# Float32r products whose columns are taken in blocks of sixteen from both halves of the operand in turn

## The chip, the cores and the metric

The kernel runs on one core of a Trainium2 chip. The metric is the time of one execution on the device, in microseconds (us). The core has five engines that run side by side and meet only through semaphores: TensorE (PE in the profile; its weight loads are listed apart, as PEld), VectorE (DVE), ScalarE (ACT), GpSimd (POOL) and SyncE (SP), which issues the transfers.

## The reference

What is computed is a stack of transformer blocks over 256 tokens of width 1024, all in float32. A first block has two layers: one with a gated linear recurrence (`hgrn2_mixer`), one with differential attention (`diff_attn_mixer`), each followed by a squared-ReLU feed-forward of width 4096. A second block has one layer: a mixer that joins a low-rank attention with a short gated convolution, a gated feed-forward of width 2816, and a gated embedding. Nearly all arithmetic is in products of this kind:

```python
def squared_relu_mlp(h, w_up, w_down):
    u = jax.nn.relu(h @ w_up)
    return (u * u) @ w_down

# second block, one layer
h = rmsnorm(x, mix_pre_norm[i])
z = h @ w_in[i]
...
f = (jax.nn.silu(h @ w_gate[i]) * (h @ w_up[i])) @ w_down[i]
x = x + rmsnorm(f, ffn_post_norm[i])
```

## The kernel before

**How a product is computed.** Every weight matrix is read from memory once, in pieces of 128 rows by 1024 columns that land in `w_raw` (4 buffers). ScalarE rounds a piece to the type float32r (`w_hi`, L1424), and VectorE subtracts to get what the rounding left over (`w_lo`, L1990); both have 5 buffers. The activations are kept in the same two parts side by side: in `xs` (and in `us`, `xs_b`, `xs_m`, `xs_s`, which serve other stages) one tile of 128 rows has 512 columns, of which the first 256 are the high parts of the 256 tokens and the last 256 the low parts. A product of a 128x128 tile of weights with the tokens is then three products of float32r: high weights by high tokens, high weights by low tokens, and low weights by high tokens. The three are added up in PSUM (`ps`, 8 banks of 512 columns). A float32r product has 256 or 512 columns; TensorE loads the 128x128 stationary operand ahead of each one.

**The forms of it.** `quantum` is the inner piece. For most layers (`kind == "feat"`) the high-weight products stand in two forms: `both_halves` (L649) takes all 512 columns with one weight load, `one_half` (L657) takes the two halves of 256 columns one after the other with two weight loads. L660 is the low-weight product. How many of the high-weight products are 512 wide is set by the table `WIDE` (L226). The other kinds, "direct" (L676 to L678), "one_bank" (L682 to L684), "one_bank_tok" (L689 to L691) and "tok" (L695 to L697), have 256 columns only. In the tok kinds the operands change places: the tokens are stationary, and the weights are the moving operand. `high_records` and `low_records` (L609, L610, L617) serve the first units of a stage. `short_tile` (L1143 to L1145), the products of `kr` (L1130 to L1132), of `ukv` (L1189 to L1191) and of `ple` (L1270 to L1272) are the same three products on other operands. The built program has 6162 float32r products of 256 columns and 579 of 512 that read their columns in a row.

**Other products.** Sums of squares, scores and turned tiles are products of plain float32: L826, L904, L917, L936, L949 to L952 are such. The profile has two records for each, since the engine passes over it twice, and each record has a weight load of its own. Two of them don't read their columns in a row: L917 reads `hq_both` in pairs or singly, with jumps, and writes with steps of 2 or 4 columns into PSUM; L936 reads runs of 4, 8 or 16 columns with as many left out between them.

**Where the operands lie.** A tensor starts at a multiple of 64 bytes, and most tensors are a multiple of 128 bytes long. `w_hi`, `w_lo`, `h` and `mo` start at an even multiple of 64 bytes. Ahead of `xs` stands a gap of 64 bytes (`HALF_PERIOD`), so that `xs` starts at an odd multiple; so do all tensors of the arena: `us`, `xs_b`, `xs_m`, `xs_s`, and also `hk`, `hq_both`, `ple_hi` and `ple_lo`. A product's first column is always at a multiple of 512 bytes from its tensor's start.

```python
w_hi = sb("w_hi", [P, SLOTS, QCOLS], F32R)
w_lo = sb("w_lo", [P, SLOTS, QCOLS], F32R)
h = sb("h", [P, KT, S])
top[0] += HALF_PERIOD
xs = sb("xs", [P, KT, 2 * S], F32R)
top[0] += HALF_PERIOD
mo = sb("mo", [P, KT, S])
```

**What sets the order.** The order of each engine's work is written out by hand. TensorE goes through the list `STREAM` unit by unit; it waits for the converted weights (`lo_ready`), for the tokens (`xs_ready`, `xs_hi`) and for PSUM banks to be taken (`pair_summed`). When it is done with a buffer it counts up `w_used`, which lets ScalarE and VectorE convert the next piece, and so the next transfer start.

Of the kernel before, what the change touches and what calls it, by code (L numbers as in the profile page):

```python
# [17 lines left out]
P = 128  # L18
D = 1024
S = 256  # L20
KT = D // P
# [207 lines left out]
def layered_kernel(nc, a, out):  # L229

    ctx = ExitStack()
    with ctx:
# [14 lines left out]
        w_hi = sb("w_hi", [P, SLOTS, QCOLS], F32R)  # L247
# [352 lines left out]
        def _(pe):  # L600
            mm = nc.tensor.matmul

            def high_records(s, kt, x, kind, pset):

                hi, lo = (w[:, s, kt % 4 * 2 * P:(kt % 4 + 1) * 2 * P] for w in (w_hi, w_lo))
                for n in range(2):
                    w = slice(n * P, (n + 1) * P)
                    o_ap = ps[:, 2 * pset + n, 0:S] if kind == "feat" else ps[:, pset, n * S:(n + 1) * S]
                    mm(o_ap, hi[:, w], x[:, kt, 0:S], start=kt == 0 and (kind == "feat" or n == 0), stop=False)  # L609
                    mm(o_ap, lo[:, w], x[:, kt, 0:S], start=False, stop=False)  # L610

            def low_records(s, kt, x, kind, pset):

                hi = w_hi[:, s, kt % 4 * 2 * P:(kt % 4 + 1) * 2 * P]
                for n in range(2):
                    o_ap = ps[:, 2 * pset + n, S:2 * S] if kind == "feat" else ps[:, pset, n * S:(n + 1) * S]
                    o = mm(o_ap, hi[:, n * P:(n + 1) * P], x[:, kt, S:2 * S], start=False,  # L617
                           stop=kt == KT - 1 and (kind == "feat" or n == 1))
                return o

# [20 lines left out]
            def quantum(s, kt0, nk, last_kt, x, kind, pset, kk0=0, tiles=(0, 1), wide=0, wide_first=False):  # L641

                hi, lo = w_hi[:, s, :].rearrange("p (k n) -> p k n", k=4), w_lo[:, s, :].rearrange("p (k n) -> p k n", k=4)
                if kind == "feat":
                    steps = [(kk, n) for kk in range(kk0, kk0 + nk) for n in tiles]

                    def both_halves(some):
                        for kk, n in some:
                            o = mm(ps[:, 2 * pset + n, :], hi[:, kk, n * P:(n + 1) * P], x[:, kt0 + kk, :],  # L649
                                   start=kt0 + kk == 0, stop=kt0 + kk == last_kt)  # L650
                        return o

                    def one_half(some):
                        for kk, n in some:
                            for half in range(2):
                                at = slice(half * S, (half + 1) * S)
                                mm(ps[:, 2 * pset + n, at], hi[:, kk, n * P:(n + 1) * P], x[:, kt0 + kk, at], start=False,  # L657
                                   stop=False)
                        for kk, n in steps:
                            o = mm(ps[:, 2 * pset + n, 0:S], lo[:, kk, n * P:(n + 1) * P], x[:, kt0 + kk, 0:S], start=False,  # L660
                                   stop=False)
                        return o

                    if wide_first:
                        both_halves(steps[:wide])
                        return one_half(steps[wide:])
                    one_half(steps[:-wide])
                    return both_halves(steps[-wide:])
                for kk in range(kk0, kk0 + nk):
                    kt = kt0 + kk  # L670
                    first, last = kt == 0, kt == last_kt
                    for n in tiles:
                        bank = 2 * pset + n
                        if kind == "direct":
                            w = slice(n * P, (n + 1) * P)
                            mm(ps[:, bank, 0:S], hi[:, kk, w], x[:, kt, 0:S], start=first, stop=False)  # L676
                            mm(ps[:, bank, 0:S], hi[:, kk, w], x[:, kt, S:2 * S], start=False, stop=False)  # L677
                            o = mm(ps[:, bank, 0:S], lo[:, kk, w], x[:, kt, 0:S], start=False, stop=last)  # L678
                        elif kind == "one_bank":
                            w = slice(n * P, (n + 1) * P)  # L680
                            at = slice(n * S, (n + 1) * S)
                            mm(ps[:, pset, at], hi[:, kk, w], x[:, kt, 0:S], start=first and n == 0, stop=False)  # L682
                            mm(ps[:, pset, at], hi[:, kk, w], x[:, kt, S:2 * S], start=False, stop=False)  # L683
                            o = mm(ps[:, pset, at], lo[:, kk, w], x[:, kt, 0:S], start=False, stop=last and n == 1)  # L684
                        elif kind == "one_bank_tok":
                            xh = x[:, kt, n * P:(n + 1) * P]
                            xl = x[:, kt, S + n * P:S + (n + 1) * P]
                            at = slice(n * S, (n + 1) * S)
                            mm(ps[:, pset, at], xh, hi[:, kk, :], start=first and n == 0, stop=False)  # L689
                            mm(ps[:, pset, at], xh, lo[:, kk, :], start=False, stop=False)  # L690
                            o = mm(ps[:, pset, at], xl, hi[:, kk, :], start=False, stop=last and n == 1)  # L691
                        else:
                            xh = x[:, kt, n * P:(n + 1) * P]
                            xl = x[:, kt, S + n * P:S + (n + 1) * P]
                            mm(ps[:, bank, 0:S], xh, hi[:, kk, :], start=first, stop=False)  # L695
                            mm(ps[:, bank, 0:S], xh, lo[:, kk, :], start=False, stop=False)
                            o = mm(ps[:, bank, 0:S], xl, hi[:, kk, :], start=False, stop=last)  # L697
                return o

            def first_two(name, x, waits, mid=None):  # L700
# [422 lines left out]
            for part in range(2):  # L1123
                g0 = 2 * UNIT0["kr"] + part
                pe.wait_ge(lo_ready, g0 + 1)
                khi, klo = (w[:, g0 % SLOTS, :].rearrange("p (k n) -> p k n", k=4) for w in (w_hi, w_lo))
                for kk in range(4):
                    kt = 4 * part + kk
                    o_ap = ps[:, MIX_BANK["kr"], 0:S]
                    mm(o_ap, khi[:, kk, 0:P], xs[:, kt, 0:S], start=(kt == 0), stop=False)  # L1130
                    mm(o_ap, khi[:, kk, 0:P], xs[:, kt, S:2 * S], start=False, stop=False)
                    o = mm(o_ap, klo[:, kk, 0:P], xs[:, kt, 0:S], start=False, stop=(kt == KT - 1))  # L1132
                o.then_inc(w_used, 1)

            sums("mix_pre")
# [4 lines left out]
            def short_tile(name, kt, cols, bank, n, xi, first, last):  # L1140
                s = (2 * UNIT0[name] + kt) % SLOTS
                o_ap, xk = ps[:, bank, n * S:(n + 1) * S], xs_s[:, xi + kt, :]
                mm(o_ap, w_hi[:, s, cols], xk[:, 0:S], start=first, stop=False)  # L1143
                mm(o_ap, w_hi[:, s, cols], xk[:, S:2 * S], start=False, stop=False)
                return mm(o_ap, w_lo[:, s, cols], xk[:, 0:S], start=False, stop=last)  # L1145

            pe.wait_ge(xs_ready, XS0["cq"] + 1)
            pe.wait_ge(lo_ready, 2 * UNIT0["uq"] + 2)
# [33 lines left out]
            for m in range(2):  # L1182
                if m == 1:
                    pe.wait_ge(z_dve, BY_DVE["uq3"])
                for kt in range(2):
                    s = (2 * UNIT0["ukv"] + kt) % SLOTS
                    xh, xl = (xs_s[:, 2 + kt, S * i + m * P:S * i + (m + 1) * P] for i in range(2))
                    o_ap, cols = ps[:, UV_BANK[m], :], slice(AH * NOPE, QCOLS)
                    mm(o_ap, xh, w_hi[:, s, cols], start=(kt == 0), stop=False)  # L1189
                    mm(o_ap, xh, w_lo[:, s, cols], start=False, stop=False)  # L1190
                    o = mm(o_ap, xl, w_hi[:, s, cols], start=False, stop=(kt == 1))  # L1191
                if m == 0:
                    o.then_inc(small_ready, 1)
                else:
# [69 lines left out]
            def ple_tiles(j, tiles, kts=(0, 1)):  # L1264
                for n in tiles:
                    cols = slice((2 * j + n) * P, (2 * j + n + 1) * P)
                    o_ap = ps[:, PLE_BANK[j], n * S:(n + 1) * S]
                    for kt in kts:
                        xk = xs_s[:, 4 + kt, :]
                        mm(o_ap, ple_hi[kt][:, cols], xk[:, 0:S], start=kt == 0 and n == 0, stop=False)  # L1270
                        mm(o_ap, ple_hi[kt][:, cols], xk[:, S:2 * S], start=False, stop=False)
                        o = mm(o_ap, ple_lo[kt][:, cols], xk[:, 0:S], start=False, stop=kt == 1 and n == 1)  # L1272
                if n == 1 and kt == 1:
                    o.then_inc(ple_done, 1)

# [1783 lines left out]
```

## Time and profile before

| | |
|---|---|
| median of 3 runs | 965.25 us (964.62 to 965.69) |
| span of the profiled execution, first to last instruction | 963.2 us |
| outside the span (median less span) | 2.05 us |
| TensorE busy | 952.3 us, 99% |
| TensorE's weight loads busy | 909.1 us, 94% |
| VectorE busy | 748.2 us, 78% |
| ScalarE busy | 547.7 us, 57% |
| mean granted TensorE clock | 0.999 |

The profiled execution is one of its own, and its total time isn't among the runs; its span is 2.05 us below their median. How to read the profile here: TensorE's records overlap. A product's record lasts from its start until its last result is written, while the next product starts before that. So neither the busy share nor the mean of one record tells what a product costs. What it costs is the distance from its start to the next one's, and that is read from the start times in the timeline, or from the chain that ended last, where each product is charged with the time until the next takes over.

### The profile page before, as it was taken

How to read it: one execution, taken by the hardware profiler on the slowest of the kernel's cores; microseconds unless marked ns; L12 is line 12 of the kernel's file. 1: busy time of each engine (PE TensorE's matmuls, PEld its weight loads, DVE VectorE, ACT ScalarE, POOL GpSimd, SP SyncE). 2: the span in 40 equal slices, each digit the busy share in tenths (PEclk: the TensorE clock that was granted, in tenths of full speed). 3: DMA queues.
4: the chain of work that ended last, by engine and by line, in shares of the span. 5: the costliest groups of instructions: out<-in, count | busy, mean ns of one | idle time of the engine just before them, and what ended most of it. 6: DMA issues, size and time to landing. Idle time of an engine off the chain costs nothing.

```text
span 963.2 us, 18430 instructions
## 1 busy us (share of the span) xinstructions
PE 952.3 (99%) x7530; PEld 909.1 (94%) x7530; DVE 748.2 (78%) x1129; ACT 547.7 (57%) x819; POOL 89.4 (9%) x91
## 2 busy tenths in 40 slices
PE   9999999999999999999999999999999999999998
PEld 8999999999999998999999999999999999999998
DVE  6998778978855599867987844489887998787777
ACT  6652366656454476756665544455666665556455
POOL 5334101000201000001000201001001000000000
PEclk9999999999999999999999999999999999999999
DMA  8733444766666836436476575626636467665651
GB/s 256 243 120 115 143 128 140 218 200 197 195 183 193 267 109 197 150 113 183 136 215 197 176 214 184 194 68 182 183 110 202 127 197 214 187 190 170 203 175 44
DMA packets 164723, 166.62 MB, mean 173 GB/s; under 512 B 6784, under 2 KB 162832, under 8 KB 164640
## 3 DMA queue, kind: packets, MB, share of 16 engines
q1 hardware_dynamic: 162752, 163.47, 55.5%
q0 software_dynamic: 1056, 1.19, 0.5%
q8 instruction: 60, 0.98, 0.4%
q10 hardware_dynamic: 832, 0.79, 0.4%
q14 instruction: 23, 0.19, 0.1%
HBM read 163.82 MB, written 1.08 MB: 171 GB/s over the span
## 4 chain that ended last, share of the span: by engine, by line
PE 82%; DVE 12%; issue 2%; ACT 2%; DMA 2%; SPq 0%; POOL 0%; ACTq 0%; DVEq 0%
PE ps L657 19%; PE ps L660 16%; PE ps L649 13%; DVE w_lo L1990 4%; PE ps L676 3%; PE ps L677 3%; PE ps L678 3%; PE ps L682 2%; PE ps L683 2%; PE ps L684 2%; PE ps L689 2%; PE ps L609 2%; PE ps L617 2%; PE ps L690 2%; PE ps L691 2%
## 5 line engine op out<-in xcount | busy, mean ns | idle before, releaser
L1990 DVE TENSOR_TENSOR w_lo<-w_raw,w_hi 128x1024 fp32r<-128x1024 f32 (+4 forms) x314 | 375.0, 1205 | 116.1 <-ACT w_hi L1424 110.3
L1424 ACT ACTIVATE w_hi<-w_raw 128x1024 fp32r<-128x1024 f32 x298 | 313.3, 1056 | 200.3 <-PE ps L660 47.6
L657 PE MATMUL ps<-xs,w_hi 128*128 128x256 f32 x1012 | 132.6, 277 | 0.0
L657 PEld LDWEIGHTS ps<-xs,w_hi 128*128 128x128 f32 x1012 | 127.0, 188 | 4.5
L660 PE MATMUL ps<-xs,w_lo 128*128 128x256 f32 x832 | 112.2, 277 | 0.0
L660 PEld LDWEIGHTS ps<-xs,w_lo 128*128 128x128 f32 x832 | 102.9, 188 | 0.2
L682 PE MATMUL ps<-xs,w_hi 128*128 128x256 f32 x320 | 91.4, 285 | 0.4 <-DVE w_lo L1990 0.4
L683 PE MATMUL ps<-xs,w_hi 128*128 128x256 f32 x320 | 89.3, 279 | 0.0
L684 PE MATMUL ps<-xs,w_lo 128*128 128x256 f32 x320 | 89.3, 279 | 0.0
L649 PE MATMUL ps<-xs,w_hi 128*128 128x512 f32 x326 | 85.1, 393 | 0.3 <-DVE mo L2018 0.2
L1431 ACT ACTIVATE tmp<-ps 128x512 f32<-128x512 f32 x75 | 44.5, 593 | 70.6 <-PE ps L649 62.6
L657 PE MATMUL ps<-us,w_hi 128*128 128x256 f32 x626 | 81.9, 277 | 0.0
L657 PEld LDWEIGHTS ps<-us,w_hi 128*128 128x128 f32 x626 | 78.6, 188 | 2.8
L2018 DVE TENSOR_TENSOR mo<-ps,tmp 128x512 f32<-128x512 f32 x75 | 51.6, 688 | 37.1 <-ACT tmp L1431 37.0
L2968 POOL TENSOR_TENSOR sq<-sq 128x512 f32<-128x512 f32 x12 | 20.1, 1676 | 546.0 <-ACT sq L1482 375.6
L660 PE MATMUL ps<-us,w_lo 128*128 128x256 f32 x516 | 69.3, 277 | 0.0
L649 PEld LDWEIGHTS ps<-xs,w_hi 128*128 128x128 f32 x326 | 56.6, 188 | 9.8 <-DVE mo L2018 1.5
L660 PEld LDWEIGHTS ps<-us,w_lo 128*128 128x128 f32 x516 | 63.6, 188 | 0.0
L682 PEld LDWEIGHTS ps<-xs,w_hi 128*128 128x128 f32 x320 | 60.1, 188 | 0.9 <-DVE w_lo L1990 0.6
L683 PEld LDWEIGHTS ps<-xs,w_hi 128*128 128x128 f32 x320 | 60.1, 188 | 0.2
L684 PEld LDWEIGHTS ps<-xs,w_lo 128*128 128x128 f32 x320 | 60.0, 188 | 0.0
L649 PE MATMUL ps<-us,w_hi 128*128 128x512 f32 x203 | 53.4, 395 | 0.0
(431 smaller groups left out, 1896.6 us busy)
## 6 DMA issues: line engine op xcount, KB each, us to landing
w_raw<-in_mlp_w_up SPq DMA_DIRECT2D x64, 512.0 KB, 4.2
w_raw<-in_mlp_w_down SPq DMA_DIRECT2D x64, 512.0 KB, 3.5
w_raw<-in_a_w_in SPq DMA_DIRECT2D x32, 512.0 KB, 4.3
w_raw<-in_w_gate SPq DMA_DIRECT2D x22, 512.0 KB, 3.8
w_raw<-in_w_up SPq DMA_DIRECT2D x22, 512.0 KB, 4.6
w_raw<-in_w_down SPq DMA_DIRECT2D x20, 512.0 KB, 4.4
w_raw<-in_w_kv SPq DMA_DIRECT2D x16, 512.0 KB, 4.3
w_raw<-in_w_in SPq DMA_DIRECT2D x16, 512.0 KB, 3.9
```

The lines of the kernel that those rows point to most:

```text
L649: o = mm(ps[:, 2 * pset + n, :], hi[:, kk, n * P:(n + 1) * P], x[:, kt0 + kk, :], start=kt0 + kk == 0, stop=kt0 + kk == last_kt)
L657: mm(ps[:, 2 * pset + n, at], hi[:, kk, n * P:(n + 1) * P], x[:, kt0 + kk, at], start=False, stop=False)
L660: o = mm(ps[:, 2 * pset + n, 0:S], lo[:, kk, n * P:(n + 1) * P], x[:, kt0 + kk, 0:S], start=False, stop=False)
L676: mm(ps[:, bank, 0:S], hi[:, kk, w], x[:, kt, 0:S], start=first, stop=False)
L677: mm(ps[:, bank, 0:S], hi[:, kk, w], x[:, kt, S:2 * S], start=False, stop=False)
L682: mm(ps[:, pset, at], hi[:, kk, w], x[:, kt, 0:S], start=first and n == 0, stop=False)
L683: mm(ps[:, pset, at], hi[:, kk, w], x[:, kt, S:2 * S], start=False, stop=False)
L684: o = mm(ps[:, pset, at], lo[:, kk, w], x[:, kt, 0:S], start=False, stop=last and n == 1)
L1424: o = fn(dst, raw, ACT.Copy)
L1431: o = fn(tmp[0:rows_, pset if slot is None else slot, :, :], ps[0:rows_, 2 * pset:2 * pset + 2, S:2 * S], ACT.Copy, scale=scale)
L1990: return v.tensor_tensor(d, x, y, ALU.subtract)
L2018: return v.tensor_tensor(dst, ps[0:rows_, 2 * pset:2 * pset + 2, 0:S], tmp[0:rows_, pset if slot is None else slot, :, :], ALU.add)
```

## The change

A helper `prod` takes the place of the matmul call for all float32r products named above. It gives the moving operand and the output another order of columns: with a block of 16 columns (64 bytes), it takes block 0 of the first half, block 0 of the second half, block 1 of the first half, and so on, upwards. For a product of 256 columns the two halves are 128 columns each, for one of 512 they are 256 each (the high and the low tokens). Input and output have the same order, so each column's result lands where it did. The stationary operand, the number of products, the order of all instructions, their waits and their counts are the same on every engine; no other engine's instruction differs. The plain float32 products are as before.

```diff
+TURN = 16
...
+            def in_turns(ap):
+
+                return ap.rearrange("p (k l e) -> p l k e", k=2, e=TURN)
+
+            def prod(o_ap, w, x, start, stop):
+
+                return mm(in_turns(o_ap), w, in_turns(x), start=start, stop=stop)
+
...
                     def both_halves(some):
                         for kk, n in some:
-                            o = mm(ps[:, 2 * pset + n, :], hi[:, kk, n * P:(n + 1) * P], x[:, kt0 + kk, :],
+                            o = prod(ps[:, 2 * pset + n, :], hi[:, kk, n * P:(n + 1) * P], x[:, kt0 + kk, :],
                                    start=kt0 + kk == 0, stop=kt0 + kk == last_kt)
                         return o
...
-                                mm(ps[:, 2 * pset + n, at], hi[:, kk, n * P:(n + 1) * P], x[:, kt0 + kk, at], start=False,
+                                prod(ps[:, 2 * pset + n, at], hi[:, kk, n * P:(n + 1) * P], x[:, kt0 + kk, at], start=False,
                                    stop=False)
```

All other replaced calls (L609, L610, L617, L660, L676 to L697, L1130 to L1132, L1143 to L1145, L1189 to L1191, L1270 to L1272) have the same form: `mm` becomes `prod`, with the same arguments.

## Rows read from the trace of the kernel before

**Rows 1.** The page: TensorE's load and its granted clock.

```profile
span 963.2 us, 18430 instructions
...
PE 952.3 (99%) x7530; PEld 909.1 (94%) x7530; DVE 748.2 (78%) x1129; ACT 547.7 (57%) x819; POOL 89.4 (9%) x91
...
PEclk9999999999999999999999999999999999999999
```

**Rows 2.** The page: the chain that ended last, by engine and line.

```profile
PE 82%; DVE 12%; issue 2%; ACT 2%; DMA 2%; SPq 0%; POOL 0%; ACTq 0%; DVEq 0%
PE ps L657 19%; PE ps L660 16%; PE ps L649 13%; DVE w_lo L1990 4%; PE ps L676 3%; PE ps L677 3%; PE ps L678 3%; PE ps L682 2%; PE ps L683 2%; PE ps L684 2%; PE ps L689 2%; PE ps L609 2%; PE ps L617 2%; PE ps L690 2%; PE ps L691 2%
```

**Rows 3.** The chain in order of time, from 224 us: start, us, what.

```profile
224.04 1.36 PE ps L657 x12
225.40 0.91 PE ps L660 x8
226.30 1.37 PE ps L649 x6
```

**Rows 4.** The same view, from 180 us.

```profile
180.31 1.41 PE ps L657 x12
181.72 0.94 PE ps L660 x8
```

**Rows 5.** Timeline of TensorE, first and last product of 256 columns with a shorter distance.

```profile
23.46 0.28 PE L684 MATMUL ps<-xs,w_lo 128*128 128x256 f32 x1
...
954.92 0.28 PE L696 MATMUL ps<-w_lo,xs 128*128 128x256 f32 x1
```

**Rows 6.** The same, first and last with a longer distance.

```profile
9.56 0.28 PE L683 MATMUL ps<-xs,w_hi 128*128 128x256 f32 x1
...
958.74 0.28 PE L697 MATMUL ps<-w_hi,xs 128*128 128x256 f32 x1
```

**Rows 7.** Timeline of TensorE: plain float32 products with columns in a row.

```profile
118.05 1.05 PE L949 MATMUL ps<-hv,acc 128*128 128x128 f32 x8
118.94 0.39 PE L951 MATMUL ps<-hv,cross 128*128 128x128 f32 x2
...
931.79 2.75 PE L826 MATMUL ps<-table 128*128 128x256 f32 x12
```

**Rows 8.** Line L826: ns min/median/max of one record.

```profile
L826 PE MATMUL ps<-table x62: 377/379/483, 157.0 to 934.2; 128*128 128x256 f32 x62
```

**Rows 9.** Timeline: plain float32 products with jumps, in what they read or write.

```profile
57.30 1.97 PE L936 MATMUL ps<-hq_both,hk 128*128 128x64 f32 x16
...
77.99 1.98 PE L917 MATMUL ps<-hq_both,hk 128*128 128x128 f32 x16
```

**Rows 10.** Lines L917 and L936: ns min/median/max of one record.

```profile
L917 PE MATMUL ps<-hq_both,hk x64: 273/275/353, 42.1 to 84.4; 128*128 128x128 f32 x64
...
L936 PE MATMUL ps<-hq_both,hk x96: 217/275/294, 52.5 to 98.1; 128*128 128x64 f32 x96
```

**Rows 11.** Timeline: float32r products on `xs_s`, weights at an even multiple of 64 bytes.

```profile
663.08 0.28 PE L1144 MATMUL ps<-xs_s,w_hi 128*128 128x256 f32 x1
...
665.67 0.28 PE L1145 MATMUL ps<-xs_s,w_lo 128*128 128x256 f32 x1
```

**Rows 12.** Timeline: float32r products on `xs_s`, weights at an odd multiple of 64 bytes.

```profile
745.34 0.28 PE L1272 MATMUL ps<-xs_s,ple_lo 128*128 128x256 f32 x1
...
746.78 0.28 PE L1272 MATMUL ps<-xs_s,ple_lo 128*128 128x256 f32 x1
```

**Rows 13.** Stretches: busy us (instructions) of PE, PEld, DVE, ACT, POOL; clock, DMA share, GB/s.

```profile
10.00:130.00 120.00, 118.72 (x1075) 117.09 (x1074) 103.67 (x152) 58.87 (x72) 36.94 (x36) 1.00 0.54 165
...
640.00:750.00 110.00, 108.08 (x846) 104.03 (x846) 94.01 (x176) 69.38 (x136) 10.19 (x8) 1.00 0.52 156
```

**Rows 14.** TensorE's largest wait: us in total, times, longest.

```profile
PE ps L830 <- DVE guess L2169: 1.2, 1, 1.2
```

More of the change, by code:

```diff
@@ L608, in high_records @@
                     o_ap = ps[:, 2 * pset + n, 0:S] if kind == "feat" else ps[:, pset, n * S:(n + 1) * S]
-                    mm(o_ap, hi[:, w], x[:, kt, 0:S], start=kt == 0 and (kind == "feat" or n == 0), stop=False)
-                    mm(o_ap, lo[:, w], x[:, kt, 0:S], start=False, stop=False)
+                    prod(o_ap, hi[:, w], x[:, kt, 0:S], start=kt == 0 and (kind == "feat" or n == 0), stop=False)
+                    prod(o_ap, lo[:, w], x[:, kt, 0:S], start=False, stop=False)
             def low_records(s, kt, x, kind, pset):
@@ L616, in low_records @@
                     o_ap = ps[:, 2 * pset + n, S:2 * S] if kind == "feat" else ps[:, pset, n * S:(n + 1) * S]
[L617 removed]
+                    o = prod(o_ap, hi[:, n * P:(n + 1) * P], x[:, kt, S:2 * S], start=False,
                            stop=kt == KT - 1 and (kind == "feat" or n == 1))
@@ L681, in quantum @@
                             at = slice(n * S, (n + 1) * S)
-                            mm(ps[:, pset, at], hi[:, kk, w], x[:, kt, 0:S], start=first and n == 0, stop=False)
-                            mm(ps[:, pset, at], hi[:, kk, w], x[:, kt, S:2 * S], start=False, stop=False)
-                            o = mm(ps[:, pset, at], lo[:, kk, w], x[:, kt, 0:S], start=False, stop=last and n == 1)
+                            prod(ps[:, pset, at], hi[:, kk, w], x[:, kt, 0:S], start=first and n == 0, stop=False)
+                            prod(ps[:, pset, at], hi[:, kk, w], x[:, kt, S:2 * S], start=False, stop=False)
+                            o = prod(ps[:, pset, at], lo[:, kk, w], x[:, kt, 0:S], start=False, stop=last and n == 1)
                         elif kind == "one_bank_tok":
@@ L688, in quantum @@
                             at = slice(n * S, (n + 1) * S)
-                            mm(ps[:, pset, at], xh, hi[:, kk, :], start=first and n == 0, stop=False)
-                            mm(ps[:, pset, at], xh, lo[:, kk, :], start=False, stop=False)
-                            o = mm(ps[:, pset, at], xl, hi[:, kk, :], start=False, stop=last and n == 1)
+                            prod(ps[:, pset, at], xh, hi[:, kk, :], start=first and n == 0, stop=False)
+                            prod(ps[:, pset, at], xh, lo[:, kk, :], start=False, stop=False)
+                            o = prod(ps[:, pset, at], xl, hi[:, kk, :], start=False, stop=last and n == 1)
                         else:
@@ L1142, in short_tile @@
                 o_ap, xk = ps[:, bank, n * S:(n + 1) * S], xs_s[:, xi + kt, :]
-                mm(o_ap, w_hi[:, s, cols], xk[:, 0:S], start=first, stop=False)
-                mm(o_ap, w_hi[:, s, cols], xk[:, S:2 * S], start=False, stop=False)
-                return mm(o_ap, w_lo[:, s, cols], xk[:, 0:S], start=False, stop=last)
+                prod(o_ap, w_hi[:, s, cols], xk[:, 0:S], start=first, stop=False)
+                prod(o_ap, w_hi[:, s, cols], xk[:, S:2 * S], start=False, stop=False)
+                return prod(o_ap, w_lo[:, s, cols], xk[:, 0:S], start=False, stop=last)
             pe.wait_ge(xs_ready, XS0["cq"] + 1)
@@ L1188, in _ @@
                     o_ap, cols = ps[:, UV_BANK[m], :], slice(AH * NOPE, QCOLS)
-                    mm(o_ap, xh, w_hi[:, s, cols], start=(kt == 0), stop=False)
-                    mm(o_ap, xh, w_lo[:, s, cols], start=False, stop=False)
-                    o = mm(o_ap, xl, w_hi[:, s, cols], start=False, stop=(kt == 1))
+                    prod(o_ap, xh, w_hi[:, s, cols], start=(kt == 0), stop=False)
+                    prod(o_ap, xh, w_lo[:, s, cols], start=False, stop=False)
+                    o = prod(o_ap, xl, w_hi[:, s, cols], start=False, stop=(kt == 1))
                 if m == 0:
```

26 lines of the change are left out of this document (13 added, 13 removed).

## Prediction

> **What bounds the kernel now.** I read the page first, for the load of the engines and the chain that ended last, then the chain in order of time and the timeline of TensorE, for what one product costs. TensorE is busy 99% of the span at full granted clock (2.4 GHz) and VectorE 78% [rows 1]; 82% of the chain is TensorE, nearly all of it float32r products [rows 2]. TensorE hardly waits: its largest wait, summed by line, is 1.2 us [rows 14]. So the time is the number of products times the distance from one product's start to the next, plus the seams between stages. The change touches that distance and nothing else.
>
> **What a product costs now.** Around 224 us twelve products of 256 columns take 1.36 us of the chain, 113.3 ns each, and six of 512 columns 1.37 us, 229 ns each [rows 3]. Around 180 us the same lines take 1.41 us for twelve, 117.8 ns each, and 0.94 us for eight [rows 4]. The products are the same; only the stretch differs. Over the whole timeline, 3579 distances after a product of 256 columns are of the shorter kind (112 to 115 ns, sum 405.6 us, mean 113.3; first and last in [rows 5]), and 2484 of the longer one (116 to 125 ns, sum 292.7 us, mean 117.8; first and last in [rows 6]). 564 distances after a product of 512 columns sum to 129.4 us, mean 229.4 ns. Together that is 828 of the 963 us.
>
> **What the floor is.** 256 columns at 2.4 GHz are 106.7 ns and 512 are 213.3 ns, so the float32r products lose 6.6 to 11 ns and 16 ns. Plain float32 products lose less. Twelve records at L826 span 2.75 us, of which the last record is 0.38 us [rows 7, 8]: 2.37 us for eleven distances, 215.5 ns, 2.2 ns over their 213.3 ns (256 columns, each for two clocks). Eight records of 128 columns stand 0.89 us before the next line [rows 7]: 111.3 ns each. Sixteen of 64 columns, half the streaming, still take 1.97 us less a last record of 0.275 us, for fifteen distances 113.0 ns [rows 9, 10]. Since halving the columns saves nothing, about 111 ns is what the weight load allows, and a product of 256 columns can't go below it. A product of 512 columns could go to 215.5 ns.
>
> **Why the float32r products miss that floor.** They read their moving operand at one column per clock, twice as fast as the plain ones, while the next weights are loaded at the plain pace (128 columns in about 107 ns). Two facts suggest that the two readings get in each other's way by address. First, plain products, where both read at the same pace, show nothing of it. Second, twelve distances at L1270 to L1272, where tokens and weights both start at an odd multiple of 64 bytes, are 1.44 us, 120.0 ns each [rows 12]; 22 distances on the same `xs_s` with weights at an even multiple are 2.59 us, 117.7 ns each [rows 11]. So the place within 128 bytes matters. My theory: a 64-byte half of each 128 bytes can serve only one of the two readings at a time. Now the tokens change halves every 16 columns (6.7 ns) and the weights every 16 columns at half the pace (13.3 ns), so they meet in each. With the change the tokens stay in one half for 32 columns, 13.3 ns, then in the other: both change at the same pace, and starting in opposite halves (`xs` odd, `w_hi` even) they needn't meet.
>
> **The change part by part.** Removed: the row-by-row order of 6162 products of 256 columns and 579 of 512. Added: 15 jumps within the first kind, 31 within the second, in the reading and in the writing. Nothing is moved: instructions, waits and queues are the same. No engine other than TensorE does more or less.
>
> The cost of the jumps at full pace isn't in the trace. The nearest rows are plain products. L917 jumps after every column or pair, in reading and writing: 1.98 us less 0.275 us for fifteen distances, 113.7 ns, against 111.3 ns in a row; L936, with runs of 4 to 16 columns, 113.0 ns with a first distance that has a seam in it [rows 7, 9, 10]. So jumps far denser than the new ones cost 0 to 2.4 ns. The price of a product of 256 columns afterwards is bounded below by 111.3 ns (the floor) and above by 120.0 ns (the worst meeting of two readings that the trace shows). I take 112.5 ns, midway between the floor and L917's 113.7 ns, since the theory removes the meetings and the jumps cost at most that. For 512 columns the bounds are 215.5 and 2 x 120.0 = 240 ns; I take 220 ns, the floor and twice the 2.4 ns.
>
> The sum: 3579 x (113.3 - 112.5) = 2.9 us, 2484 x (117.8 - 112.5) = 13.2 us, 564 x (229.4 - 220) = 5.3 us, together 21.4 us. What is late next is VectorE's `w_lo`: it is busy 103.7 of 120 us and 94.0 of 110 us in the two stretches that hold most of the longer kind [rows 13], 86% and 85%. With TensorE 4.5% faster there this becomes 90% and 89%, still below TensorE, but short waits will appear; I take 1.5 us for them, an estimate. 963.2 - 19.9 = 943.3 us of span, and with 2.05 us outside it 945.3 us. With all terms at their lower bounds: 3579 x 2.0 + 2484 x 6.5 + 564 x 13.9 = 7.2 + 16.1 + 7.8 = 31.1 us, 934 us. If the shorter kind can't improve and 512 columns gain 5 ns only: 11.2 + 2.8 = 14 us, 951 us.
>
> The rows on jumps bear on a rule of the Trainium skill, Advanced Engine Details and Errata, section PSUM Cachelines: "Any non-contiguous AP significantly slows down matmuls", though the next line asks only that every two consecutive elements lie together, which the new order keeps. L917 writes with steps and pays 2.4 ns, so this trace does not bear the strong reading out, at half pace at least. By the strong reading the sum would turn positive; it is the second rival.
>
> **The rivals.**
>
> *The readings meet more, not less* (slower). The theory needs the weights to be in the other half at the moment the tokens are. Which half the load of the next weights is in when a product begins the trace doesn't show. If they start in the same one, both now walk at the same pace and meet all along, or one is held back at each product until they are apart. This decides in every product at once. For it: opposite starts are no guarantee, and 120.0 ns stands in [rows 12]. Price at 120.0 ns: 3579 x 6.7 + 2484 x 2.2 + 564 x 10.6 = 24.0 + 5.5 + 6.0 = 35.5 us, 1001 us; a weaker form, where all products fall into the longer kind of 117.8 ns, costs 3579 x 4.5 = 16.1 us, 981 us.
>
> *The jumps cost and nothing is gained* (slower). At L917's 2.4 ns for each 256 columns on top of today's distances: 6162 x 2.4 + 579 x 4.8 = 17.6 us, 983 us; it could be more, since the rows are at half pace. For it: no row shows jumps at full pace. Against it: the new blocks are 8 to 16 times longer than L917's runs.
>
> *It does not do what it says* (no change). What the float32r products lose may have nothing to do with the order of columns: a fixed loss by stretch, and a weight load that bounds the short ones. Then 965 us, within 2 us. For it: 113.3 ns is only 2 ns above the floor of the weight load. Against it: 229 ns for 512 columns, where the weight load has time to spare [rows 3], and the 120.0 ns of [rows 12].
>
> On this the Trainium skill, TensorE: Matmul & The Clock Gate, section Step-by-step: what each phase is for, says that TensorE has two independent read ports, one for the streamed operand and one for the weights. By it they could not meet, and the order would not matter: this rival. The trace disagrees as far as 120.0 against 117.7 ns goes, which differ by the weights' address.
>
> **How the numbers follow.** Likeliest, the meetings go: 0.56, 934 to 951 us, 945 us. No change: 0.12. More meetings: 0.20, spread over 981 to 1001 us. Jumps cost: 0.12, from 975 us up. About 0.2% is what a measurement of this kernel tells from no change. So faster 0.56, same 0.12, slower 0.32. The range of 936 to 992 us leaves out a little below and the worse halves of both slower cases, less than 0.2 together.
>
> **What would show it.** In the timeline of the changed kernel twelve L657 products should take 1.34 to 1.36 us, everywhere, without a longer kind; six of 512 columns under 1.33 us. The products of L1270 to L1272, which start in the same half, should do worse than the others: if they do better, it is the starting halves that I have wrong. L826, L917 and L949 must stay at 215.5, 113.7 and 111.3 ns. A float32r distance at 117.8 or 120 ns everywhere proves the first slower rival; one that grows with the number of jumps, 512 columns by twice as much as 256, the second; a VectorE wait of TensorE of over 5 us would show that the gain was given back.

## The result: 997.1 us, 3.3% slower

| | before | after |
|---|---|---|
| median | 965.5 us (4 runs) | 997.1 us (996.9 to 997.3, 4 runs) |
| ratio | | 1.0326 (95%: 1.0312 to 1.0341) |
| span of the profiled execution | 963.2 us | 995.4 us |
| TensorE busy | 952.3 us, 99% | 986.6 us, 99% |
| VectorE busy | 748.2 us | 748.5 us |
| mean granted TensorE clock | 0.999 | 0.999 |

The page of the kernel after answers [rows 1]. The clock is the same, the other engines did the same work, and TensorE is busy 34 us longer:

```profile
span 995.4 us, 18430 instructions
...
PE 986.6 (99%) x7530; PEld 940.9 (95%) x7530; DVE 748.5 (75%) x1129; ACT 549.3 (55%) x819; POOL 89.5 (9%) x91
...
PEclk9999999999999999999999999999999999999999
```

All float32r products now come from one line of the helper, L610; the products of plain float32 moved down by 9 lines. The timeline of TensorE after, around the place of [rows 3]: start, us, line, tiles, form, count.

```profile
228.32 1.12 PE L610 MATMUL ps<-xs,w_lo 128*128 128x256 f32 x8
229.28 1.60 PE L610 MATMUL ps<-xs,w_hi 128*128 128x256 f32 x12
230.72 1.12 PE L610 MATMUL ps<-xs,w_lo 128*128 128x256 f32 x8
```

Eight products take 0.96 us from their start to the next row's, twelve take 1.44 us: 120.0 ns each, where twelve took 1.36 us in [rows 3] and 1.41 us in [rows 4]. The two kinds of stretch are gone; 5491 of 5998 distances between two products of 256 columns are exactly 120 ns, and 459 of 475 between two of 512 are exactly 240 ns. The products of `ple`, at 120.0 ns in [rows 12], are where they were:

```profile
767.39 0.29 PE L610 MATMUL ps<-xs_s,ple_lo 128*128 128x256 f32 x1
...
769.55 0.29 PE L610 MATMUL ps<-xs_s,ple_lo 128*128 128x256 f32 x1
```

Eighteen distances in 2.16 us are 120.0 ns. The sum closes: distances without a wait after products of 256 columns grew from 698.4 us (6063 of them) to 728.0 us (6066), those of 512 columns from 129.4 (564) to 137.5 us (573), those with a wait or a seam in them fell from 32.0 to 25.6 us. That is 29.6 + 8.1 - 6.4 = 31.3 us of the 32.2 us by which the span grew.

### The profile page after: what moved, and what is told of

Its sections match the earlier page's. It is cut to its first block, busy times and chain, and to the rows that moved or that the text cites. A ratio compares the mean times of both kernels' runs of the same rounds, so it can differ in the third digit from the quotient of the medians.

```text
span 995.4 us, 18430 instructions
## 1 busy us (share of the span) xinstructions
PE 986.6 (99%) x7530; PEld 940.9 (95%) x7530; DVE 748.5 (75%) x1129; ACT 549.3 (55%) x819; POOL 89.5 (9%) x91
## 4 chain that ended last, share of the span: by engine, by line
PE 87%; DVE 9%; issue 2%; ACT 1%; DMA 1%; POOL 0%; ACTq 0%; DVEq 0%
PE ps L610 79%; DVE w_lo L1999 2%; PE ps L945 1%; DVE mo L2117 1%; PE ps L1047 1%; DVE xs L2147 1%; PE ps L926 1%; DMA relb<-in_rel_bias 1%; PE ps L839 0%; PE ps L1055 0%; PE ps L819 0%; DVE xs_b L2132 0%; PE ps L1237 0%; PE ps L1212 0%; DVE sq L2104 0%
## 5 line engine op out<-in xcount | busy, mean ns | idle before, releaser
L1433 ACT ACTIVATE w_hi<-w_raw 128x1024 fp32r<-128x1024 f32 x298 | 313.3, 1056 | 220.3 <-PE ps L610 198.0
L610 PE MATMUL ps<-xs,w_hi 128*128 128x256 f32 (+1 forms) x2410 | 415.5, 300 | 1.1 <-ACT xs L1525 1.1
L610 PEld LDWEIGHTS ps<-xs,w_hi 128*128 128x128 f32 x2410 | 357.4, 191 | 18.9 <-issue 2.4
L610 PE MATMUL ps<-xs,w_lo 128*128 128x256 f32 x1368 | 262.8, 283 | 0.0
L610 PEld LDWEIGHTS ps<-xs,w_lo 128*128 128x128 f32 x1368 | 209.6, 191 | 0.2
L610 PE MATMUL ps<-us,w_hi 128*128 128x256 f32 (+1 forms) x1173 | 197.4, 304 | 0.0
L610 PEld LDWEIGHTS ps<-us,w_hi 128*128 128x128 f32 x1173 | 172.1, 191 | 10.1
L610 PE MATMUL ps<-us,w_lo 128*128 128x256 f32 x688 | 120.9, 283 | 0.0
L610 PEld LDWEIGHTS ps<-us,w_lo 128*128 128x128 f32 x688 | 99.3, 191 | 0.0
L610 PE MATMUL ps<-w_hi,xs 128*128 128x256 f32 x288 | 56.2, 288 | 0.0
L610 PEld LDWEIGHTS ps<-w_hi,xs 128*128 128x128 f32 x288 | 45.9, 190 | 0.2
L610 PE MATMUL ps<-xs_b,w_hi 128*128 128x256 f32 (+1 forms) x249 | 45.8, 289 | 0.0
L610 PE MATMUL ps<-w_lo,xs 128*128 128x256 f32 x144 | 40.8, 283 | 0.0
L610 PEld LDWEIGHTS ps<-xs_b,w_hi 128*128 128x128 f32 x249 | 38.5, 191 | 0.8 <-issue 0.3
L610 PE MATMUL ps<-xs_b,w_lo 128*128 128x256 f32 x128 | 32.9, 283 | 0.0
L610 PEld LDWEIGHTS ps<-w_lo,xs 128*128 128x128 f32 x144 | 27.4, 190 | 0.0
```

What stands on the lines that cost most here:

```text
L610: return mm(in_turns(o_ap), w, in_turns(x), start=start, stop=stop)
L1433: o = fn(dst, raw, ACT.Copy)
```

## The experiments

Two theories stood after the result. **M**, the one of the prediction: the tokens' reading and the loading of the weights meet in one 64-byte half of 128 bytes, and now all along. **J**: each jump or block of the moving operand costs, whatever the weights do; 120.0 = 106.7 + 16 x 0.83 ns and 240.0 = 213.3 + 32 x 0.83 ns, one clock of 1.2 GHz per block, spoke for it. Unless it says otherwise, a time below is that of a single run, beside one run of the kernel before of 965.4 to 965.7 us; a distance is the mean over all of the kernel's distances of that kind without a wait or a seam in them.

### Other block lengths: 32 and 8

```diff
-TURN = 16
+TURN = 32
```

> The changed kernel with blocks of 32 columns in place of 16. Its float32r distances were 120.0 ns for 256 columns and 240.0 ns for 512 everywhere, which is 106.7 + 16 x 0.83 and 213.3 + 32 x 0.83 ns: one clock of 1.2 GHz for each block. Theory J (each block of a jumping order costs one such clock): 8 and 16 blocks, 113.3 and 226.7 ns everywhere, span 995.4 - 6162 x 6.67 ns - 579 x 13.3 ns = 947 us. Theory M (tokens and weights meet in the same 64-byte half of 128 bytes): blocks of 32 columns change halves every 16 columns, just as columns in a row do, so 113 to 118 ns and 229 ns again, span 963 us. If it stays at 120.0 ns, any jumping order costs the same.

Measured: 990.3 us, span 988.5 us; a product of 256 columns 119.0 ns on average (115 to 124), one of 512 columns 236.8 ns. Twelve products take 1.43 us here:

```profile
227.91 1.59 PE L610 MATMUL ps<-xs,w_hi 128*128 128x256 f32 x12
229.34 1.11 PE L610 MATMUL ps<-xs,w_lo 128*128 128x256 f32 x8
```

```diff
-TURN = 16
+TURN = 8
```

> The changed kernel with blocks of 8 columns. Theory J: twice the blocks, 106.7 + 32 x 0.83 = 133.3 ns for 256 columns and 266.7 ns for 512, span 995.4 + 6162 x 13.3 ns + 579 x 26.7 ns = 1093 us. Theory M: a half of 128 bytes is still left after 32 columns, as with blocks of 16, so 120.0 and 240.0 ns stay, span 995 us.

Measured: 1016.4 us, span 1014.6 us; 123.3 ns and 243.3 ns. Ten products take 1.23 us:

```profile
226.97 1.40 PE L610 MATMUL ps<-xs,w_hi 128*128 128x256 f32 x10
228.20 1.15 PE L610 MATMUL ps<-xs,w_lo 128*128 128x256 f32 x8
```

Both theories fall in their simple form. Halving or doubling the number of blocks moves the loss beyond 106.7 ns from 13.3 ns to 12.3 and 16.6 ns, where J wanted 6.7 and 26.7 ns; M wanted 113 to 118 ns and 120.0 ns.

### Reading alone, writing alone

```diff
-                return mm(in_turns(o_ap), w, in_turns(x), start=start, stop=stop)
+                return mm(o_ap, w, in_turns(x), start=start, stop=stop)
```

> The changed kernel, but only the reading takes the blocks in turn; the results are written in a row, so the columns of each product come out in another order than they should (its output is not the reference's). If the price lies in the reading (J in the reading, or M): 120.0 and 240.0 ns, span 995 us. If it lies in the writing to PSUM: as before the change, 113 to 118 ns and 229 ns, span 963 us.

Measured: 997.1 us, 120.0 and 240.0 ns, as in the changed kernel. Twelve products take 1.44 us:

```profile
229.04 1.60 PE L610 MATMUL ps<-xs,w_hi 128*128 128x256 f32 x12
230.48 1.12 PE L610 MATMUL ps<-xs,w_lo 128*128 128x256 f32 x8
```

```diff
-                return mm(in_turns(o_ap), w, in_turns(x), start=start, stop=stop)
+                return mm(in_turns(o_ap), w, x, start=start, stop=stop)
```

> The changed kernel, but only the writing to PSUM takes the blocks in turn; the reading is in a row (its output is not the reference's, since columns come out in another order). If the price lies in the reading: 113 to 118 ns and 229 ns, span 963 us. If it lies in the writing: 120.0 and 240.0 ns, span 995 us.

Measured: 966.2 us, span 964.4 us; both kinds of distance are back, 113 and 118 ns. The timeline of this kernel, where eight products take 0.91 us and then 0.90 us to the next row's start:

```profile
225.77 1.07 PE L610 MATMUL ps<-xs,w_lo 128*128 128x256 f32 x8
226.68 2.44 PE L610 MATMUL ps<-xs,w_hi 128*128 128x512 f32 x14
228.96 1.07 PE L610 MATMUL ps<-xs,w_lo 128*128 128x256 f32 x8
229.87 1.07 PE L610 MATMUL ps<-xs,w_hi 128*128 128x256 f32 x8
```

So the whole price lies in the reading, and writing blocks of 64 bytes into PSUM in another order costs nothing that one run can show. The rule of the Trainium skill that the prediction weighed (Advanced Engine Details and Errata, section PSUM Cachelines: "Any non-contiguous AP significantly slows down matmuls") does not hold here in its strong reading: 966.2 us against 965.4 us.

### Blocks of 16 in other orders

```diff
-                return ap.rearrange("p (k l e) -> p l k e", k=2, e=TURN)
+                return ap.rearrange("p (l k e) -> p l k e", k=2, e=TURN)[:, :, ::-1, :]
```

> Blocks of 16 columns again, a jump at the end of each as in the changed kernel, but only neighbours change places: block 1, 0, 3, 2, and so on. So the reading jumps just as often, and leaves a 64-byte half after every 16 columns, as columns in a row do. Theory J' (a jump in the reading costs, wherever it goes): 120.0 and 240.0 ns, span 995 us. Theory H (the price is for staying in one 64-byte half of 128 bytes for 32 columns, while the weights are read at half the pace): 113 to 118 ns and 229 ns, span 963 us, as in a row.

Measured: 984.5 us, span 982.7 us; with the tokens as the moving operand 117.9 ns (115 to 120) and 234.9 ns.

```profile
226.90 1.58 PE L610 MATMUL ps<-xs,w_hi 128*128 128x256 f32 x12
228.31 1.11 PE L610 MATMUL ps<-xs,w_lo 128*128 128x256 f32 x8
```

```diff
-                return ap.rearrange("p (k l e) -> p l k e", k=2, e=TURN)
+                return ap.rearrange("p (l e) -> p l e", e=TURN)[:, ::-1, :]
```

> Blocks of 16 columns, the last block first and so on down to the first, upwards within a block. The halves alternate after every 16 columns as in a row, and every block ends in a jump back. J': 120.0 and 240.0 ns, 995 us. H: 113 to 118 ns and 229 ns, 963 us; since which of the two readings is ahead may change with the direction, the share of the two kinds may change, 955 to 975 us.

Measured: 994.9 us, span 993.1 us; 120.0 ns (118 to 122, tokens moving) and 237.7 ns. All three kernels have the same number of jumps, and 512 columns take 234.9, 237.7 and 240.0 ns: it matters where a jump goes. But neither comes back to the times of columns in a row, though both leave a half after every 16 columns, so "halves of 128 bytes" is not it either.

### Weights moved by 64 bytes

```diff
+        top[0] += HALF_PERIOD
         w_hi = sb("w_hi", [P, SLOTS, QCOLS], F32R)
         w_lo = sb("w_lo", [P, SLOTS, QCOLS], F32R)
+        top[0] += HALF_PERIOD
```

Once with columns in a row (`prod` passes its operands as they are), once with turns of 16. The weights move by 64 bytes and the tokens, which lie behind both gaps, by 128.

> Columns in a row as before the change, but w_hi and w_lo moved by 64 bytes, so that weights and tokens both start at an odd multiple of 64 bytes, as at L1270 to L1272 of before, where 120.0 ns was read. If the place of the two readings against each other sets the distance (my theory, and H): 120 ns for 256 columns nearly everywhere in the layers, span 985 to 995 us. If it doesn't, and 120.0 ns there had another cause: 113 to 118 ns and 963 us.

Measured: 987.7 us, span 985.8 us; 119.0 ns (112 to 124) and 232.7 ns. Where weights and tokens lie does matter for columns in a row: 22 us. (By 256 bytes, the period found further down, the tokens start here 32 columns past the weights and not at the same place, as they do in [rows 12]; a stretch at 32 took 118.7 ns.)

> The changed kernel with w_hi and w_lo moved by 64 bytes. If in the changed kernel tokens and weights are read in the same half all along because of where they start, as the slower rival has it, this puts them in opposite halves: 111 to 113 ns, below 950 us. If they fall in step by themselves wherever they start, or if the price is for the jumps (J'): 120.0 and 240.0 ns again, 995 us.

Measured: 997.5 us, span 995.7 us; 120.0 to 120.3 ns and 239.7 ns. In turns of 16 their place doesn't matter. So putting the weights into the other half would not have brought the forecast gain, and the rival "the readings start in the same half" is not what happened.

### Stretches of products alone, after all other work

The decisive measurement: the kernel before, with stretches of equal products appended to TensorE's program, behind a wait for the last copies out of PSUM. VectorE, ScalarE and GpSimd have no instruction there. The form of a stretch:

```diff
+            for i in range(32):
+                mm(turns(16)(ps[0:32, 0, 0:512]), w_even(i, 32), turns(16)(x_of(i, 512)), start=False, stop=False)
```

`w_even` is a tile of `w_hi`, `w_odd` one of `xs`, `x_of` the first columns of a tile of `xs`. In many stretches the distances differ over the first few products and then repeat; where a distance "settles", it is that of the later ones.

> The kernel before, with stretches of 32 float32r products each added at its very end, when every other engine is idle; the kernel's own part is unchanged, the time grows by the stretches. 512 columns in a row and in turns of 16, each with weights of 128 and of 32 columns (a load of a quarter of the length); the same with 256 columns; with weights at an odd multiple of 64 bytes; and turns of 8, 32, 64 and swapped neighbours with weights of 32 columns. Theory L (what the products lose is lost to the loading of the weights, which is read beside the tokens): with weights of 32 columns a product of 512 falls from 229 to about 219 ns in a row and from 240 to about 222 ns in turns, since the load is there for a quarter as long, and the difference between the orders falls to a quarter. Theory S (the reading of the tokens pauses by itself, whatever is loaded): 226 to 229 ns and 240 ns with either, and turns of 8, 32 and 64 as in the whole kernels (243, 237). If idle VectorE, ScalarE and transfers matter, 512 columns in a row with weights of 128 differ from the 229 ns of the kernel.

The timeline of TensorE at its end; L1387 is in a row, L1389 in turns, both with weights of 128 columns, L1391 and L1393 the same with 32; L1395 to L1401 the same four with 256 columns; L1403 and L1405 are 512 columns in a row and in turns with weights at an odd multiple of 64 bytes.

```profile
971.67 7.49 PE L1387 MATMUL ps<-xs,w_hi 128*128 128x512 f32 x32
978.99 7.84 PE L1389 MATMUL ps<-xs,w_hi 128*128 128x512 f32 x32
986.67 7.58 PE L1391 MATMUL ps<-xs,w_hi 128*32 128x512 f32 x32
994.09 7.84 PE L1393 MATMUL ps<-xs,w_hi 128*32 128x512 f32 x32
1001.77 3.94 PE L1395 MATMUL ps<-xs,w_hi 128*128 128x256 f32 x32
1005.55 4.01 PE L1397 MATMUL ps<-xs,w_hi 128*128 128x256 f32 x32
1009.39 3.82 PE L1399 MATMUL ps<-xs,w_hi 128*32 128x256 f32 x32
1013.04 4.00 PE L1401 MATMUL ps<-xs,w_hi 128*32 128x256 f32 x32
1016.89 7.43 PE L1403 MATMUL ps<-xs 128*128 128x512 f32 x32
1024.16 7.84 PE L1405 MATMUL ps<-xs 128*128 128x512 f32 x32
```

What one costs is the distance between the starts of two rows over the count: with 512 columns 7.32 / 32 = 229 ns in a row and 240 ns in turns; with weights of a quarter of the columns 232 ns and 240 ns. With 256 columns in turns, 120 ns with 128 columns of weights and 3.85 / 32 = 120 ns with 32. The load was indeed shorter: its record is 188 ns with 128 columns (L1387) and 108 ns with 32 (L1391). Theory L falls and S holds: the reading of the tokens loses time by itself, however long the weights' load is, and whether or not other engines work. In turns of 16 the weights change nothing. In a row they do: 256 columns take 117.8 ns with 128 columns of weights and settle at 113.3 ns with 32; 512 columns settle at 226.7 ns when the weights are a tile of `xs` too (L1403), against 228.9 ns (L1387).

Here the Trainium skill, TensorE: Matmul & The Clock Gate (section Step-by-step: what each phase is for), was nearer than my theory: by its two independent ports the length of the load should not matter, and it didn't. But where the weights lie against the tokens should not matter by it either, and that moved a whole kernel by 22 us.

### Which block after which

> Again the kernel before with stretches of 24 float32r products of 512 columns added at its end, all with weights of 32 columns, reading w_lo in different patterns and writing in a row: in a row from five starts; blocks of 16 columns at distances of 0, 32, 48, 64, 80, 96, 112, 128 and 144 columns and backwards; runs of 2 to 64 columns with as much left out between; blocks of 16 from two places 64, 80, 128, 240, 256 and 272 columns apart in turn; one column 512 times. Last, plain float32 in a row and in turns of 16. Theory N (a jump costs, wherever it goes): all patterns with blocks of 16 columns take the same 240 ns, runs of 32 about 237 ns, of 64 about 231 ns. Theory B (it depends on which block is read next after which, as it would if neighbouring 64-byte blocks lay in different banks and a bank needed time): blocks of 16 at an odd number of blocks' distance (48, 80, 112, 144, and pairs 80, 240, 272 apart) are like columns in a row, 227 to 233 ns, those at an even number (0, 32, 64, 96, 128, and pairs 64, 128, 256 apart) at 240 ns or more. Plain float32: 215.5 ns for both orders in either theory, since it reads at half the pace.

In the timeline, each row is one pattern of 24 products of 512 columns, weights of 32 columns. L1373 and L1375 read in a row, from columns 0 and 16; L1383 the same block of 16 columns 32 times; L1385 to L1399 read blocks at a distance of 32, 48, 64, 80, 96, 112, 128 and 144 columns; L1401 is L1385 started 16 columns later; L1415 reads blocks in turn from two places 256 columns apart, as the changed kernel does. L1431 and L1433 are plain float32 in a row and in turns.

```profile
970.72 5.72 PE L1373 MATMUL ps<-w_lo,w_hi 128*32 128x512 f32 x24
976.28 5.73 PE L1375 MATMUL ps<-w_lo,w_hi 128*32 128x512 f32 x24
...
998.38 6.02 PE L1383 MATMUL ps<-w_lo,w_hi 128*32 128x512 f32 x24
1004.24 5.88 PE L1385 MATMUL ps<-w_lo,w_hi 128*32 128x512 f32 x24
1009.96 5.77 PE L1387 MATMUL ps<-w_lo,w_hi 128*32 128x512 f32 x24
1015.56 6.03 PE L1389 MATMUL ps<-w_lo,w_hi 128*32 128x512 f32 x24
1021.43 5.71 PE L1391 MATMUL ps<-w_lo,w_hi 128*32 128x512 f32 x24
1026.97 5.92 PE L1393 MATMUL ps<-w_lo,w_hi 128*32 128x512 f32 x24
1032.72 5.77 PE L1395 MATMUL ps<-w_lo,w_hi 128*32 128x512 f32 x24
1038.33 6.03 PE L1397 MATMUL ps<-w_lo,w_hi 128*32 128x512 f32 x24
1044.19 5.71 PE L1399 MATMUL ps<-w_lo,w_hi 128*32 128x512 f32 x24
1049.74 5.92 PE L1401 MATMUL ps<-w_lo,w_hi 128*32 128x512 f32 x24
...
1094.35 5.92 PE L1415 MATMUL ps<-w_lo,w_hi 128*32 128x512 f32 x24
1100.11 5.92 PE L1417 MATMUL ps<-w_lo,w_hi 128*32 128x512 f32 x24
...
1139.78 5.37 PE L1431 MATMUL ps<-h,table 128*32 128x256 f32 x24
1144.98 5.34 PE L1433 MATMUL ps<-h,table 128*32 128x256 f32 x24
```

Averaged over all distances of a stretch but its first two:

| step from block to block, modulo 4 blocks (256 bytes) | distances, in columns | ns per 512 columns |
|---|---|---|
| 1 (as in a row) | 16, 80, 144 | 231.5, 230.8, 230.8 |
| 3 | 48, 112, -16 | 233.5, 233.6, 233.3 |
| 2 | 32, 96 | 238.3, 240.0 |
| 0 (the same place) | 0, 64, 128 | 244.1, 244.2, 244.2 |

N falls: steps of different length cost from 230.8 to 244.2 ns. B was right that the step decides, but its period was not: steps alike modulo 256 bytes take the same time within 2 ns, and steps alike modulo 128 bytes need not (48 against 80 columns by 3 ns, 32 against 64 by 6). B was wrong for the pairs as well: it wanted 227 to 233 ns for 80, 240 and 272 columns apart, and blocks in turn from two places 64, 80, 128, 240, 256 and 272 columns apart all took 240.0 ns. Each of these orders has a step of 0 or of 2 blocks in it, on the way there or back. The changed kernel's is one of them: 8 blocks on and 7 back with 256 columns, 16 on and 15 back with 512, steps 0 and 1. In the earlier stretches, swapped neighbours have steps of 3 only and took 233.3 ns, turns of 64 have steps of 1 only and took 231.2 ns, as the table has it. Turns of 32 have one step of 3 in four and took 236.6 ns, more than the table gives, and so did runs of 32 columns with 32 left out, whose steps are 1 and 3 in turn; so the steps don't simply add. The start counts too: steps of 32 columns took 238.3 ns from column 0 and 240.0 ns from column 16 (L1401), and columns in a row from column 8 took 226.6 ns against 231.5 ns from 0. Plain float32 settled at 215.8 ns both in a row and in turns (L1431, L1433): at half the pace the turned order costs nothing.

### The weights' place within 256 bytes

> The kernel before with stretches at its end again, now with full weights of 128 columns: 48 products of 256 columns in a row whose first column lies 0, 8, 16, 24, 32, 48 or 4 columns past a multiple of 64 (32 bytes are 8 columns), 32 products of 512 columns from 0, 8, 16 and 24, and 48 of 256 in turns of 16 from 0 and 8. Weights start at an even multiple of 64 bytes. The last stretches showed four places that repeat every 64 columns, and columns in a row from column 8 at 226.7 ns where other starts took 230 to 232 ns. If that holds with full weights, 256 columns from 8 and 24 take 113.3 ns throughout, and the tokens belong at 32 bytes; if the weights' load sets it, 113.3 and 117.8 ns come back at 16 and 48, 120 ns at 0 and 32. In turns of 16 the price is 120.0 ns from 0; a start at 8 puts two places into each block, which by the four places is between the orders, 113 to 120 ns.

The timeline; L1373 to L1383 are 256 columns in a row whose start lies 0, 8, 16, 24, 32 and 48 columns from the weights' place, L1385 is 4, and L1387 is 512 columns at 0.

```profile
970.26 5.92 PE L1373 MATMUL ps<-w_lo,w_hi 128*128 128x256 f32 x48
976.02 5.82 PE L1375 MATMUL ps<-w_lo,w_hi 128*128 128x256 f32 x48
981.68 5.82 PE L1377 MATMUL ps<-w_lo,w_hi 128*128 128x256 f32 x48
987.33 5.91 PE L1379 MATMUL ps<-w_lo,w_hi 128*128 128x256 f32 x48
993.08 5.86 PE L1381 MATMUL ps<-w_lo,w_hi 128*128 128x256 f32 x48
998.78 5.62 PE L1383 MATMUL ps<-w_lo,w_hi 128*128 128x256 f32 x48
1004.23 5.76 PE L1385 MATMUL ps<-w_lo,w_hi 128*128 128x256 f32 x48
1009.83 7.44 PE L1387 MATMUL ps<-w_lo,w_hi 128*128 128x512 f32 x32
```

5.76 / 48 = 120.0 ns at 0; 116.7 at 4; 117.8 at 8 and at 16; 119.8 at 24; 118.7 at 32; and at 48 it settles at 113.3 ns. The tokens and weights of [rows 12], with their 120.0 ns, lie at 0 as well. The expectation that 8 or 24 would be best was wrong. So is any rule of one best place: 0, the worst for 256 columns, is the best of the four tried for 512, where it settles at 226.7 ns (L1387), against 233.3 ns at 8, 228.9 ns at 16 and 233.4 ns at 24; 48 was not tried with 512. In turns of 16 it was 120.0 ns from 0 and from 8. In the kernel before, tokens lie 16 columns past the weights. 48 was to be had by moving the weights by 128 bytes:

```diff
+        top[0] += 2 * HALF_PERIOD
         w_hi = sb("w_hi", [P, SLOTS, QCOLS], F32R)
         w_lo = sb("w_lo", [P, SLOTS, QCOLS], F32R)
+        top[0] += 2 * HALF_PERIOD
```

> The kernel before, columns in a row, with w_hi and w_lo moved by 128 bytes, so that the tokens start 48 columns (192 bytes) past the weights modulo 64 columns, where they started 16 columns past them. In the last stretches 48 products of 256 columns took 113.4 ns at that place and 117.8 ns at the old one. If the place within 256 bytes carries over to the layers: the 2484 longer distances (117.8 ns) turn into 113.3 ns, 11 us less, about 954 us and faster; the products of 512 columns may move by a few ns either way (564 of them, 2 us). If only places within 128 bytes count, as I had it in the prediction, nothing changes: 965 us. The products where weights are the moving operand (L689 to L691, some 400) see the reverse distance, 16, and stay.

Measured, medians of 8 and of 11 runs: 968.5 us against 965.9 us, ratio 1.0026 (1.0015 to 1.0037). By distances about a fifth of what was expected came true: the longer kind (117.9 ns) fell only from 2484 to 2003, where nearly all were to go. At the start of the program, where the kernel before had 117.8 ns, it is 113.4 ns, though the tokens, moved by 256 bytes, start at the same place modulo 256 as before, so there it is the weights' place that counts. Of the one_bank products (L682 to L684) 377 are of the longer kind where 929 were. But the products of kind direct (L676 to L678), which read high and low weights and tokens in the same order, from tensors at the same places, went the other way: before, 611 of 660 were of the shorter kind, now none. So the place alone doesn't set the kind. Moreover, products of 512 columns went from 229.4 to 232.5 ns, and distances with a wait or a seam in them grew from 32.0 to 35.6 us: -2.4 us, +1.2 us and +3.6 us, and about 1.1 us elsewhere. So it is slower by a quarter of a percent. That the place within 128 bytes is not enough is shown, since that was left as it was; a better kernel was not found.

## Why the prediction was wrong

- **What bounds the kernel, and that the change acts through the distance alone: right.** The other engines' work is unchanged, and TensorE's distances carry 31.3 of 32.2 us. No wait of TensorE came up: its largest is 1.2 us again.
- **The floor from the weights' load, 111 ns: not tested for float32r**, since nothing came near it. A row of the kernel before speaks for it: with weights of 64 columns, sixteen plain products of 64 columns stand 58 to 59 ns apart once they are under way, where weights of 128 columns took 113.0 ns for the same 64 columns (L936). But the load is not what holds float32r products in a row at 113.3 ns, since in the first stretches they settle there with a quarter of the weights too (L1399). In the changed kernel the plain products stayed where the prediction put them (L826, there L835: 215.5 ns forecast, 215.8 measured).

```profile
70.34 1.15 PE L926 MATMUL ps<-hq_both,hk 128*64 128x64 f32 x16
```

- **The step that failed is the theory of what the float32r products lose.** The prediction took the loss for a meeting of tokens and weights in halves of 128 bytes, from two facts. The first, that plain products show nothing, is as well explained by their half pace in the moving operand alone: in the appended stretches, with weights of 32 columns, the turned order costs them nothing (215.8 ns) and float32r products of 512 columns 8 ns (231.9 to 240.0 ns). The second, 120.0 against 117.7 ns by the weights' place, was a true effect, but it modifies the loss and is not its source: with a quarter of the weights the loss in turns is the same. And its period is not 128 bytes. The row that should have warned was in the argument: with 512 columns the weights are loaded for less than half of the product, yet the loss is more than twice that with 256 columns at 113.3 ns [rows 3]. A loss to the weights would not grow with the columns.
- **The bounds were right, the choice within them wrong.** The upper bounds, 120.0 and 240 ns, are to the tenth what was measured, and the slower rival's 1001 us is 4 us from the 997 us found; most of the 4 are waits and seams that shrank, which its price left out. But its mechanism is not what happened: moving the weights by 64 bytes leaves 120.0 ns, and so does a quarter of the weights. So its near hit was luck, and one of the prediction's own signs misled: it said that 120 ns everywhere would prove this rival, and 120 ns everywhere came without it.
- **The price of a jump at full pace**, taken from L917 and L936 at half pace, 0 to 2.4 ns, was mis-sized. The changed kernel pays 4.8 ns on average for 256 columns (115.2 to 120.0 ns) and 10.6 ns for 512. It is no price of a jump at all: a jump to a block at 1 modulo 4 is free, one to the same place costs the most. Rows of products that read at half the pace could bound nothing here.
- **The range** ended at 992 us and left out the worse half of a rival to which 0.20 was given, while that rival's price at 120.0 ns was 1001 us. The changed kernel gave one price nearly everywhere, not a spread.

Open: that the order of the reading causes the loss is shown, but what in the chip repeats after 256 bytes is not; four banks that each need time would fit the table, but no run tests for them. Open too are why steps of 0 and 1 in turn cost 240.0 ns where their mean would be 237.5 ns; why blocks backwards took 237.7 ns in the whole kernel and 233.3 ns in a stretch with 32 columns of weights; and why products in a row fall into two regular kinds, 113.3 and 117.8 ns.

## What to carry to other kernels

The time of a float32r product depends on the order in which it reads its moving operand: read columns in a row, or in an order whose steps between 64-byte blocks are 1 modulo 4 (231 ns for 512 columns in the stretches, in a row or with such steps). An order that comes back to the same place modulo 256 bytes in every other step took 240 ns, 8 to 13 ns more than columns in a row with the same weights, and one that comes back in every step 244 ns. To find who causes a loss on TensorE, append stretches of one product each to a kernel, vary the columns of the one operand and then of the other, and see with which the loss grows. And take a price at full pace only from rows at full pace.

## What else the runs showed of the hardware

- Runs of 2 columns with 2 left out between cost 452 ns per 512 columns (11.04 us for 24 products), runs of 4 with 4 left out 230.6 ns, as in a row.

```profile
1061.10 11.04 PE L1405 MATMUL ps<-w_lo,w_hi 128*32 128x512 f32 x24
1071.94 5.74 PE L1407 MATMUL ps<-w_lo,w_hi 128*32 128x512 f32 x24
```

- Reading one column 512 times costs 218.6 ns, the nearest to 213.3 ns that a float32r product of 512 columns came.
- A whole kernel of columns in a row changes by 22 us (965.6 to 987.7 us) when the weights move by 64 bytes and the tokens by 128, with no instruction changed but for its addresses.
